# The order of weight columns and of tokens in TensorE's operands, stage by stage

## The reference, cut to what matters

```
# first block (mixers and attention before this)
hm = rms_norm(x, norm_mlp) @ mlp_w1            # 1024 -> 4096
x = x + square(relu(hm)) @ mlp_w2              # 4096 -> 1024
# second block
proj = rmsnorm(x, ln1_g) @ w_in                # 1024 -> 7 x 1024
...                                            # convolutions, a gated linear recurrence
merged = sigmoid(...) * (y_a @ w_out_a) + sigmoid(...) * (y_b @ w_out_b)
x = x + merged @ w_o
h = rmsnorm(x, ln2_g)
x = x + (silu(h @ w_ffn_gate) * (h @ w_ffn_up)) @ w_ffn_down   # 1024 -> 2816 -> 1024
```

## Time and profile before

| | |
|---|---|
| median of 2 runs | 1629.48 us (1629.29 to 1629.67) |
| span of the profiled execution, first to last instruction | 1626.4 us |
| time of that execution outside the span, by the median | 3.1 us |
| TensorE's granted clock, mean over the span | 0.997 of full |
| PE busy / PEld busy / DVE / ACT | 98% / 81% / 56% / 42% of the span |

### The profile page before, as it was taken

One profiled execution on the slowest core, in us unless ns is written; L12 is line 12 of the kernel. 1 busy time (PEld: TensorE's weight loads), 2 busy tenths in 40 slices (PEclk: granted clock), 3 DMA queues, 4 the chain that ended last, 5 costly groups with the idle time before them and its releaser, 6 DMA issues.

```text
span 1626.4 us, 21588 instructions
## 1 busy us (share of the span) xinstructions
PE 1595.6 (98%) x7524; PEld 1311.0 (81%) x7524; DVE 912.4 (56%) x1319; ACT 684.1 (42%) x996; POOL 157.1 (10%) x97
## 2 busy tenths in 40 slices
PE   6999999999999999999999999999999999999997
PEld 5888798788788888888888888888888888888886
DVE  4549799765664323444377666666455544444332
ACT  5735554554653213433244545554224434443221
POOL 3445486100000000000000000000000000000000
PEclk9999999999999999999999999999999999999999
DMA  7521100122123232233233333333322323222332
GB/s 286 165 78 65 52 1 2 65 86 96 40 91 103 91 103 90 90 104 103 59 105 106 93 93 93 93 93 104 104 90 91 104 90 102 91 93 86 99 97 77
DMA packets 45665, 149.50 MB, mean 92 GB/s; under 512 B 4784, under 2 KB 5936, under 8 KB 45616
## 3 DMA queue, kind: packets, MB, share of 16 engines
q1 hardware_dynamic: 42240, 139.90, 27.1%
q10 hardware_dynamic: 3376, 8.95, 1.5%
HBM read 146.47 MB, written 2.10 MB: 91 GB/s over the span
## 4 chain that ended last, share of the span: by engine, by line
PE 91%; DVE 6%; DMA 1%; ACT 1%; issue 0%; ACTq 0%; DVEq 0%; SPq 0%
PE acc L627 84%; DVE c_acc L2105 1%; DVE tok L2243 1%; DMA x<-xT 1%; DVE d_score_a L2246 1%; PE acc L938 1%; DVE d_score_b L2246 1%; PE acc L963 1%; PE acc L1113 0%; PE acc L1134 0%; DVE g_x L2229 0%; PE acc L800 0%; PE acc L702 0%; DVE w_lo L1973 0%; DVE x L2681 0%
## 5 line engine op out<-in xcount | busy, mean ns | idle before, releaser
L627 PE MATMUL acc<-h_hi,w_hi 128*128 128x512 f32 x1248 | 492.3, 394 | 1.4 <-issue 0.8
L627 PE MATMUL acc<-h_hi,w_lo 128*128 128x512 f32 x1248 | 491.6, 394 | 0.0
L627 PE MATMUL acc<-h_lo,w_hi 128*128 128x512 f32 x1248 | 488.7, 392 | 0.0
L1981 DVE TENSOR_TENSOR w_lo<-raw,w_hi 128x1024 fp32r<-128x1024 f32 (+2 forms) x241 | 281.5, 1171 | 81.7 <-ACT w_hi L1384 59.7
L1384 ACT ACTIVATE w_hi<-raw 128x1024 fp32r<-128x1024 f32 (+2 forms) x241 | 241.9, 1007 | 178.2 <-PE acc L627 86.4
L627 PEld LDWEIGHTS acc<-h_hi,w_hi 128*128 128x128 f32 x1248 | 234.8, 188 | 54.3 <-issue 3.8
L627 PEld LDWEIGHTS acc<-h_lo,w_hi 128*128 128x128 f32 x1248 | 234.9, 188 | 53.4 <-issue 1.0
L627 PEld LDWEIGHTS acc<-h_hi,w_lo 128*128 128x128 f32 x1248 | 234.9, 188 | 49.2
L627 PE MATMUL acc<-u_hi,w_hi 128*128 128x512 f32 x256 | 100.9, 394 | 0.0
L627 PE MATMUL acc<-u_hi,w_lo 128*128 128x512 f32 x256 | 100.4, 392 | 0.0
L2384 DVE TENSOR_TENSOR x<-x,acc 128x512 f32 x32 | 22.0, 688 | 139.2 <-PE acc L627 138.7
(11 more groups left out here) (394 smaller groups left out, 2323.1 us busy)
## 6 DMA issues: line engine op xcount, KB each, us to landing
raw<-panels_a SPq DMA_DIRECT2D x112, 512.0 KB, 3.3
raw<-panels_b SPq DMA_DIRECT2D x68, 512.0 KB, 3.3
raw<-mix SPq DMA_DIRECT2D x48, 448.0 KB, 3.4
raw<-mix SPq DMA_DIRECT2D x16, 512.0 KB, 3.7
raw<-down SPq DMA_DIRECT2D x16, 384.0 KB, 3.2
raw<-down SPq DMA_DIRECT2D x16, 320.0 KB, 2.9
x<-xT ACTq DMA_DIRECT2D x4, 1024.0 KB, 9.5
x_rows<-xN ACTq DMA_DIRECT2D x2, 1024.0 KB, 8.6
```

Of the source, the lines that this page charges most:

```text
L627: mm = e.matmul(out, w[:, w_at:w_at + wn], a, start=first and n == 0, stop=last and n == 2)
L1981: TTn(lo, raw, k.w_hi[:, ahead.slot(w)].bitcast(F32), ALU.subtract).then_inc(k.s_split_done, 1)
```

## The change

In every dense stage from up0 on but mix, the 128 columns of a stationary block are no longer side by side. The host lays the blocks of a panel out in groups of n: column j of the group's block b lies at j*n + b. `stationary` reads a block with a step of n, so that the same weights reach the same array columns. And where the second entry of `ORDER` is True, the moving operand and the output are both walked from the last token to the first, so that each token's result still lands in its own place.

```
+ORDER = {"front": (1, False), "up0": (1, True), "dn0": (2, True), "up1": (4, True), "dn1": (4, False), "mix": (1, False), "merge": (2, False), "w_o": (8, True), "ffn": (8, False), "down": (6, True)}
...
+def stationary(w, slot, block, blocks, order):
+    n, _ = order
+    g = block // n * n
+    n = min(n, blocks - g)
+    a = slot + g * P + block - g
+    return w[:, a:a + (P - 1) * n + 1:n]
+
+def turned_back(ap, order):
+    return ap[:, ::-1] if order[1] else ap
...
-    def products(out, w_at, wn, a_hi, a_lo, first, last):
+    def products(out, slot, block, a_hi, a_lo, first, last, order, blocks=KT):
         for n, (w, a) in enumerate(((k.w_hi, a_hi), (k.w_hi, a_lo), (k.w_lo, a_hi))):
-            mm = e.matmul(out, w[:, w_at:w_at + wn], a, start=first and n == 0, stop=last and n == 2)
+            mm = e.matmul(turned_back(out, order), stationary(w, slot, block, blocks, order), turned_back(a, order), start=first and n == 0, stop=last and n == 2)
         return mm
...
+def ordered(p, order):
+    n, _ = order
+    out, blocks = [], p.shape[2] // P
+    for g in range(0, blocks, n):
+        b = p[:, :, g * P:min(g + n, blocks) * P].reshape(p.shape[0], P, -1, P)
+        out.append(b.transpose(0, 1, 3, 2).reshape(p.shape[0], P, -1))
+    return out[0] if len(out) == 1 else np_concatenate(out)
...
-    panels_a = cat([wk, wv, panels(w_in), panels(a["w_out"][0]), panels(a["xa_wq"][0]), wo,
-                    up[:MTH], dn[0], up[MTH:], dn[1]], 0)
+    fr = lambda p: ordered(p, ORDER["front"])
+    panels_a = cat([fr(wk), wv, fr(panels(w_in)), fr(panels(a["w_out"][0])), fr(panels(a["xa_wq"][0])), fr(wo),
+                    ordered(up[:MTH], ORDER["up0"]), ordered(dn[0], ORDER["dn0"]), ordered(up[MTH:], ORDER["up1"]),
+                    ordered(dn[1], ORDER["dn1"])], 0)
```

More of the change, by code:

```diff
@@ L640, in panel @@
                 e.wait_ge(ready[0], ready[1] + t + 1)
-            mm = products(out, slot + (at + n) * P, P, hi[:, t * w:(t + 1) * w], lo[:, t * w:(t + 1) * w],
-                          first and n == 0, last and n == len(tiles) - 1)
+            mm = products(out, slot, at + n, hi[:, t * w:(t + 1) * w], lo[:, t * w:(t + 1) * w],
+                          first and n == 0, last and n == len(tiles) - 1, order, blocks)
         if done:
@@ L1218, in tensor_program @@
     for j in range(2, 4):
-        panel(acc.take(e, j)[:], k.h_hi, k.h_lo, range(KT))
+        panel(acc.take(e, j)[:], k.h_hi, k.h_lo, range(KT), order=ORDER["up0"])
     for half in range(2):
@@ L1225, in tensor_program @@
             for j in range(4):
-                panel(acc.take(e, j % 2)[:], k.h_hi, k.h_lo, range(KT))
+                panel(acc.take(e, j % 2)[:], k.h_hi, k.h_lo, range(KT), order=ORDER[f"up{half}"])
             pan.leave(MTH // 4 - (half == 0))
@@ L1234, in tensor_program @@
                 ready = (k.s_up_lo, MTH * half)
-                panel(out, k.u_hi, k.u_lo, range(0, 8), last=False, ready=ready)
-                panel(out, k.u_hi, k.u_lo, range(8, 16), first=False, ready=ready)
+                panel(out, k.u_hi, k.u_lo, range(0, 8), last=False, ready=ready, order=ORDER[f"dn{half}"])
+                panel(out, k.u_hi, k.u_lo, range(8, 16), first=False, ready=ready, order=ORDER[f"dn{half}"])
             pan.leave(KT // 2)
@@ L1261, in mix_tile @@
                 out = acc.take(e, bank) if first else k.ps[bank]
-                mm = products(out[:], slot + (n - a) * P, P, til(hi, t), til(lo, t), first, last)
+                mm = products(out[:], slot, n - a, til(hi, t), til(lo, t), first, last, ORDER["mix"], b - a)
             mm.then_inc(k.s_panel_used, 1)
@@ L1289, in tensor_program @@
         t = KT - 1
[L1290 removed]
+        products(k.ps[n][:], slots[n], t, til(hi, t), til(lo, t), False, True, ORDER["merge"]).then_inc(k.s_panel_used, 1)
     for n, (hi, lo) in enumerate(both):
[L1292 removed]
+        panel(acc.take(e, 2 + n)[:], hi, lo, range(KT), order=ORDER["merge"])
     with e.Fori(0, KT // 2 - 1) as i:
@@ L1297, in tensor_program @@
             for n, (hi, lo) in enumerate(both):
-                panel(acc.take(e, 2 * j + n)[:], hi, lo, range(KT))
+                panel(acc.take(e, 2 * j + n)[:], hi, lo, range(KT), order=ORDER["merge"])
         pan.leave(KT // 2 - 1)
@@ L1306, in tensor_program @@
         for j in range(4):
-            panel(acc.take(e, j % 2)[:], k.mg_hi, k.mg_lo, range(KT), ready=(k.s_mg_lo, 0))
+            panel(acc.take(e, j % 2)[:], k.mg_hi, k.mg_lo, range(KT), ready=(k.s_mg_lo, 0), order=ORDER["w_o"])
         pan.leave(2)
@@ L1312, in tensor_program @@
     for j in range(4):
-        panel(acc.take(e, j)[:], k.h_hi, k.h_lo, range(KT), ready=(k.s_fed_lo, 5 * KT))
+        panel(acc.take(e, j)[:], k.h_hi, k.h_lo, range(KT), ready=(k.s_fed_lo, 5 * KT), order=ORDER["ffn"])
         if j == 0:
@@ L1319, in tensor_program @@
         for j in range(4):
-            panel(acc.take(e, j)[:], k.h_hi, k.h_lo, range(KT))
+            panel(acc.take(e, j)[:], k.h_hi, k.h_lo, range(KT), order=ORDER["ffn"])
         pan.leave(FFN // 2 - 1)
```

21 lines of the change are left out of this document (13 added, 8 removed).

## The result

The changed kernel takes 1662.98 us (median of 2, 1662.73 to 1663.23) where the kernel before takes 1629.48 us: 1.0206 times as long, 95% interval 1.0187 to 1.0225. So it is slower than before beyond the noise; whether by more than 2% is open, since the interval holds 1.02. The profiled execution has a span of 1660.9 us against 1626.4 us.

What follows compares the result with a forecast made beforehand. The prediction took TensorE, in an unbroken run of matmuls at 228.9 ns, as the bound. Its terms, 0 + 0 + 0 with up to 1 us of uncovered loads, left 1630 us, range 1580 to 1740.

Steps and rivals of the forecast that it cites:

- the likeliest case, no change: Whole kernel: the same loads and matmuls keep one pace of 228.9 ns, so 1630 us; chance 0.65.
- Both signs of being wrong: The prediction's own tests: it is wrong if a backward stream costs anything, or a stepped load is over twice as long.
- the forecast's own range: Whole kernel if nothing changes: 1626 to 1636 us.
- E: Strided loads and stream disturb one another in the stepped stages: 10 us plus 33 to 99 us, 1672 to 1739 us; chance 0.11.
- the three zeros of the sum: Changed stages: stepped stationary blocks, moving operand read backwards and output written backwards were each taken as 0 us.
- Item 1: Stepped stationary blocks, 768 loads at step 2, 2544 at 4 or more: 0, even twice as slow, hidden by the running matmul.
- Rival C: Strided loads outgrow the matmul hiding them, over some 220 ns: +244 us at three times, +517 at four; chance 0.09.
- Item 2: Moving operand read last token to first in up0, dn0, up1, w_o, down, 1872 matmuls: 0 taken, bounds 0 and 200 ns each.
- Item 3: Output written backwards into PSUM in the same 1872 matmuls: 0 taken, bounds 0 and 200 ns each.
- Rival B: Backwards reading or writing is slow: 1872 matmuls at 429 ns, +375 us, 2004 us; chance 0.10.
- The 15.6 ns: Every dense matmul: what is left of the 228.9 ns pace over the 213.3 ns stream of 512 columns at 2.4 GHz.
- Rival D: Faster: 13 ns vanish in each of 3696 changed matmuls where the order changes, 48 us, 1582 us; chance 0.05.

## Why the prediction was right in its range and wrong in its value

The bound was read rightly: one cadence from 445 us on, TensorE never waiting, so that only the distance between matmuls counts, and the stages as separate tests. The range of 1580 to 1740 holds 1663; the value, 1630, and the likeliest case, no change, do not hold. Both signs of being wrong came: a backward stream costs something, and a load with step 4 is over twice as long. That the range covers 1663 is luck: it lies in the gap between the forecast's own range, to 1636, and E's times, from 1672. So the three zeros of the sum stand against 34.5 us:

*Item 1, the step of the weight columns, is the step that failed*: 26.2 us. By the paces (step 1 in the same direction as reference): ffn 17.0 us, dn1 4.3, w_o 2.7, merge 1.7, down 0.5, up1 and dn0 0. It failed in two ways.

The first is the cover. A load twice as long was to be "still nothing". But it was 107 ns that I doubled, where the rows and the trace have 111 to 113 for a load beside 64 columns; twice 112 is 224, within 5 ns of the pace, and the load came out at 233 (step 4) and 238 to 242 (step 8), 2.1 to 2.2 times. (The 104 ns that I read from the last of the earlier trace rows are no faster load either: its loads start 112 ns apart as well, and only its second matmul starts 58 ns after the first.) Rival C named this place, from some 220 ns, and priced it from three times the load on. With the loads alone at 233.3 and 237.6, what sticks out of the cover is, as an estimate, 4.4 ns in dn1 (1.7 us), 8.7 in ffn (9.2 us) and 4.3 in w_o (0.8 us), together 11.7 us.

The second is the overlap itself. The other 14.5 us are what load and stream cost one another, which the sum put at nothing: merge's 1.7 us are all of this kind, since its load takes 120 ns at most. With 242 for step 8 the split is 16.7 and 9.5. This is rival E's mechanism, with 4.4 ns in merge where E had 13, and 245.8 in ffn within E's 242 to 268. E had 0.11, and its price for steps from 4 up began at 33 us, where at most 13 came. The lower bound, that a step of 0 is as fast as 1, was read where at most 128 columns streamed (the prediction says so itself under E); beside 512 columns a step of 0 costs 2.2 ns.

*Item 2, reading backwards*: not 0 and not 200 ns, but 4.4, in 1872 matmuls 8.2 us; the kernel with direction alone is 8.5 us slower. *Item 3, writing backwards*: 0, right. Rival B was right that reading backwards is slower, and wrong in size. The two items do not add: beside a load with step 2 the backward stream costs nothing more than the forward one, and beside step 4 less.

*The 15.6 ns* over the stream, which the prediction left unexplained, are 2.5 ns that remain when the moving operand repeats a token, and 13 ns that come with reading distinct tokens beside a load. Rival D, that the change of order would take them away, did not come: all changed stages got slower.

On the rules that I weighed: the section SBUF Cachelines of the Trainium skill's page "Advanced Engine Details and Errata" points the right way for the length of loads, with pairs nearly free (195 against 188 ns of record) and a new line for each column dear (309). For the moving operand it does not hold here: by that section two tokens from each 16-byte line should be enough, and they took 453.3 ns against 228.9. The section PSUM Cachelines of the same page of the Trainium skill says that patterns that are not contiguous slow matmuls down much. A step of -1 in the output did not: up0 of the run that takes backwards apart kept 228.9 ns within panels.

## What to carry to other kernels

Before calling an edit of an operand hidden, compute the slack of its cover in nanoseconds and ask for the factor at which it breaks. Here it was two for a load of 112 ns under a pace of 229, and the factor came out at 2.1. Then ask as well what the two cost one another: loads that stayed far inside their cover still cost 4.4 ns (step 2) and 6.1 ns (step 3) a matmul. In this kernel, with 512 float32r columns, the cheapest order is the plain one: tokens in whole runs of 4 neighbours, rising, and stationary columns at a step of 1. Where the tokens are walked backwards anyway (233.3 ns), steps of 2 to 4 for the stationary columns cost nothing on top. When stages differ only in a parameter, one profiled run is a table, and swapping the parameters among the stages tells the parameter from the stage.

## What was not expected of the hardware

- A forward stream of 512 float32r columns of distinct tokens takes 228.9 ns a matmul, one of repeated tokens 215.8, at 2.4 GHz.
- A load of 128 columns with step 1 takes some 112 ns at 2.4 GHz and 213.3 at 1.2 GHz; steps 2 and 3 take at most 120 and 179 at 2.4 GHz and the same 213.3 at 1.2; step 4 takes 233 at both.
- A strided load that ends long before the matmul beside it slows it all the same: 233.3 ns with step 2, whose load takes 120 at most.
- Beside a load with step 4 backwards is faster (233.3) than forwards (240.0, every second matmul 247).
- Leaving out seven eighths of the tokens of the dense stages saved 1 us: with matmuls of 64 columns the granted clock fell to 0.50, where loads with steps 1 to 3 take 213 ns, and loads with steps from 4 up take 222 to 240 ns.
- Every second token read in two passes costs 453.3 ns a matmul, every eighth in eight passes 431.1.
